# Splitting the last tiles before an output norm, and the start of the next group, into token halves

## The reference

```python
def rms_norm_2(x, gain):
    xf = x.astype(jnp.float32)
    y = xf * lax.rsqrt(jnp.mean(xf * xf, axis=-1, keepdims=True) + RMS_EPS)
    return y.astype(x.dtype) * gain

for l in range(DEPTH):
    h = rms_norm_2(x, g_pre_mix[l])
    m = hybrid_mixer(h, ...)              # ends in  y @ w_out
    x = x + rms_norm_2(m, g_post_mix[l])
    h = rms_norm_2(x, g_pre_ffn[l])
    f = conv_ffn(h, ...)                  # ends in  (gelu(gate) * up) @ w_down
    x = x + rms_norm_2(f, g_post_ffn[l])
```

## Time and profile before

| | |
|---|---|
| median of three runs | 2911.78 us |
| span of the profiled execution | 2910.6 us |
| PE matmuls | 2894.1 us (99%), 14902 |
| PE weight loads | 2395.3 us (82%) |
| DVE | 1819.4 us (63%) |
| ACT | 1275.0 us (44%) |
| POOL | 181.9 us (6%) |
| DMA | 263.90 MB, 27.3% of the engines' time on the weight queue |
| chain that ended last | PE 94%, ACT 2%, DVE 2% |

### The profile page before, as it was taken

How to read it: one execution, slowest core, us unless ns; L and a number is a source line. 1 busy time by engine, 2 the same in 40 slices (tenths; PEclk the granted TensorE clock), 3 DMA queues, 4 the chain that set the end, 5 groups by cost and what they waited for, 6 DMA issues and landing times.

```text
span 2910.6 us, 38306 instructions
## 1 busy us (share of the span) xinstructions
PE 2894.1 (99%) x14902; PEld 2395.3 (82%) x14902; DVE 1819.4 (63%) x3151; ACT 1275.0 (44%) x2352; POOL 181.9 (6%) x124
## 2 busy tenths in 40 slices
PE   9999999999999999999999999999999999999998
PEld 8888888888888888888888788888888888888886
DVE  5766775345555387733657767775365777677743
ACT  4544443333333354432356544543233765444431
POOL 1000000010000000000101301000030022100000
PEclk9999999999999999999999999999999999999999
DMA  4232333322222232232411132333233112323322
GB/s 158 76 102 95 101 96 100 95 87 80 80 85 81 95 101 95 94 101 85 144 60 44 59 102 80 102 99 97 94 106 117 38 52 73 109 76 101 98 94 73
DMA packets 74727, 263.90 MB, mean 91 GB/s; under 512 B 9009, under 2 KB 9009, under 8 KB 74417
## 3 DMA queue, kind: packets, MB, share of 16 engines
q1 hardware_dynamic: 73680, 258.03, 27.3%
q10 hardware_dynamic: 864, 3.41, 0.3%
HBM read 255.64 MB, written 2.10 MB: 89 GB/s over the span
## 4 chain that ended last, share of the span: by engine, by line
PE 94%; ACT 2%; DVE 2%; issue 1%; DMA 0%; POOL 0%; DVEq 0%; SPq 0%
PE bank L551 26%; PE bank L558 26%; PE bank L554 26%; PE bank L760 2%; PE bank L628 2%; PE bank L632 2%; PE bank L629 2%; PE bank L739 2%; PE bank L724 1%; PE bank L930 1%; DVE big L2186 1%; PE bank L715 1%; ACT pp L1157 1%; ACT big L1481 1%; PE bank L983 1%
## 5 line engine op out<-in xcount | busy, mean ns | idle before, releaser
L1502 DVE TENSOR_TENSOR wl<-ring,wh 128x512 fp32r<-128x512 f32 (+1 forms) x928 | 638.6, 694 | 804.8 <-ACT wh L1066 799.5
L551 PE MATMUL bank<-xh,wh 128*128 128x512 f32 x2392 | 943.7, 395 | 0.1
L554 PE MATMUL bank<-xh,wl 128*128 128x512 f32 x2392 | 932.7, 390 | 0.2 <-DVE wl L1502 0.2
L558 PE MATMUL bank<-xl,wh 128*128 128x512 f32 x2392 | 904.5, 390 | 0.0
L1066 ACT ACTIVATE wh<-ring 128x512 fp32r<-128x512 f32 (+1 forms) x928 | 569.1, 622 | 696.6 <-PE bank L558 622.3
L551 PEld LDWEIGHTS bank<-xh,wh 128*128 128x128 f32 x2392 | 449.8, 188 | 102.5 <-issue 10.4
L558 PEld LDWEIGHTS bank<-xl,wh 128*128 128x128 f32 x2392 | 449.3, 188 | 95.0
L554 PEld LDWEIGHTS bank<-xh,wl 128*128 128x128 f32 x2392 | 449.8, 188 | 91.1 <-DVE wl L1502 1.3
L551 PE MATMUL bank<-bigr,wh 128*128 128x512 f32 x1024 | 398.9, 390 | 0.2
L554 PE MATMUL bank<-bigr,wl 128*128 128x512 f32 x1024 | 398.4, 389 | 0.0
L558 PE MATMUL bank<-bigr,wh 128*128 128x512 f32 x1024 | 393.4, 389 | 0.0
(11 more groups left out here) (237 smaller groups left out, 2894.4 us busy)
## 6 DMA issues: line engine op xcount, KB each, us to landing
ring<-in_w_up SPq DMA_DIRECT2D x176, 512.0 KB, 3.5
ring<-in_w_down SPq DMA_DIRECT2D x88, 512.0 KB, 3.5
ring<-in_w_in SPq DMA_DIRECT2D x64, 512.0 KB, 3.6
ring<-in_w_ret SPq DMA_DIRECT2D x32, 512.0 KB, 3.6
ring<-in_w_even SPq DMA_DIRECT2D x19, 512.0 KB, 3.8
ring<-in_w_ret_v SPq DMA_DIRECT2D x16, 512.0 KB, 3.6
ring<-in_w_ret_out SPq DMA_DIRECT2D x16, 512.0 KB, 3.6
ring<-in_w_proj SPq DMA_DIRECT2D x16, 512.0 KB, 3.4
```

Of the source, the lines that this page charges most:

```text
L551: e.matmul(o, K.wh(p, c * 128, 128), oh, start=start, stop=False, skip_group_check=True)
L554: e.matmul(o, K.wl(p, c * 128, 128), oh, start=False, stop=False, skip_group_check=True)
L558: m = e.matmul(o, K.wh(p, c * 128, 128), ol, start=False, stop=stop, skip_group_check=True)
L1502: e.tensor_tensor(K.wl(i, 0, w), K.raw(i), K.wh(i, 0, w).bitcast(F32), ALU.subtract).then_inc(F.lo.tell(("piece", i)), 1)
```

## The change

- `wo` (both layers): tiles 6 and 7 are each computed in two halves of 256 tokens, in the order tile 6 first half, tile 7 first half, tile 6 second half, tile 7 second half, with the same weights twice (`post_out`). The first half's sums and spread stand inside the second halves.
- `down` (both layers): tile 7 is computed in two halves, and its weights come a second time from HBM for the second half (`post_down`).
- ACT's squares, DVE's copies, mean, POOL's root and PE's sums and spread are done for each half.
- The next group does its first three steps (`EARLY`) for the first half of the tokens, then for the second, and the rest as before (`late_group`). The second half's sums stand behind step 0 and its spread behind step 1 of the first half.
- DVE's feed of those three steps goes by halves (`early`), ACT's too.
- The matmuls on constants behind the output norms go, but for the last norm. The far-ahead splitting of pieces goes: `ahead` loses its special case, and `+ 10` becomes `+ 3` with a few pieces put between the halves.
- The last norm, its additions and the output go by halves: sixteen transfers instead of eight. Four small copies of DVE move from before a group to behind it.

The diff, cut to its core:

```diff
     def ahead(self, key):
-        if key[:2] in (("wo", 0), ("wo", 1), ("down", 2)) and key[2] > 5:
-            return self.final[key] + (5 if key[2] == 6 else 8)
         return min([self.final[key] + 3] + ...
...
-        W.stationary(D[f"w_down{f}"], 0, [("down", f, j) for j in range(DT)], FT)
+        W.stationary(D[f"w_down{f}"], 0, [("down", f, j) for j in range(DT + f // 2)], FT)
...
+    def late_group(key, operand, banks, hooks, s):
+        parts = [[take() for _ in banks] for k in range(EARLY)]
...
+        for h in range(2):
+            for k in range(EARLY):
+                oh = operand[0](k, h)[:, side(h)]
+                for m, b in enumerate(banks):
...
+                    high(BK[b][:, side(h)], *parts[k][m], oh, h == 0 and k == 0)
+                ol = operand[1](k, h)[:, side(h)]
+                for m, b in enumerate(banks):
+                    low(BK[b][:, side(h)], *parts[k][m], ol, False, last=h == 1 and parts[k][m][1] == 3)
+                if h == 0 and k == 0:
+                    half_sums(s, 1)
+                if h == 0 and k == 1:
+                    half_spread(s, 1)
+        group(key, DT, operand, banks, hooks, EARLY)
...
+    def post_out(l, operand):
...
+        for i in range(2):
+            half_tile(("wo", l, 6 + i), DT, operand, b[i], 0, [(p, c, False) for p, c in parts[i]])
+        for i, hooks in enumerate(({1: lambda: half_sums(s, 0)}, {0: lambda: half_spread(s, 0)})):
+            half_tile(("wo", l, 6 + i), DT, operand, b[2 + i], 1, [(p, c, c == 3) for p, c in parts[i]], hooks)
...
+    def post_down(l):
+        s, key = ("p", l, "f"), ("down", 2 + l, DT - 1)
+        for h, hooks in enumerate(({}, {1: lambda: half_sums(s, 0), 8: lambda: half_spread(s, 0)})):
...
# ACT, post
-        hi_to(W.final[(*key, DT - 1)] + 10)
+        p = W.final[(*key, DT - both)]
+        hi_to(W.final[(*key, DT - 1)] + 3)
+        if both:
+            half_square(s, key, DT - 2, 0)
+        half_square(s, key, DT - 1, 0)
+        hi_to(p + 4)
+        if both:
+            half_square(s, key, DT - 2, 1)
+        hi_to(p + 6)
+        half_square(s, key, DT - 1, 1)
...
# DVE, post
-        lo_to(W.final[(*key, DT - 1)] + 10)
+        lo_to(W.final[(*key, DT - 1)] + 3)
+        if both:
+            half_copy(s, key, DT - 2, 0, M)
+        half_copy(s, key, DT - 1, 0, M)
+        if not both:
+            lo_to(W.final[(*key, DT)] - 2)
+        half_mean(s, 0)
...
# DVE, post_feed (p: the next group's first piece)
+        def early():
+            if not both:
+                lo_to(p - 2)
+            half_first(0)
+            if both:
+                half_copy(s, key, DT - 2, 1, M)
+            lo_to(p - 1)
+            half_x(0, 0)
+            half_low(0, 0)
+            lo_to(p + 1)
+            half_next(1, 0)
+            lo_to(p + 3)
+            half_mean(s, 1)
+            half_copy(s, key, DT - 1, 1, M)
+            half_low(1, 0)
+            half_next(2, 0)
+            half_low(2, 0)
+            half_first(1)
+            half_x(0, 1)
+            half_low(0, 1)
+            half_next(1, 1)
+            half_next(2, 1)
+            half_low(1, 1)
+            half_low(2, 1)
```

More of the change, by code:

```diff
@@ L513, in sync_program @@
             e.dma_start(K.DIL, K.D["dil"]).then_inc(F.dil.tell("dil", by=16), 16)
[L514 to L521, removed]
+    for h in range(2):
+        for j in range(DT):
+            if j in (1, 3, 5):
+                q.wait_ge(F.pool, ("x", "end", j, h))
+            else:
+                q.wait_ge(F.dve, ("x", "end", j, h))
+            e.dma_start(K.out[:, j * S + 256 * h:j * S + 256 * h + 256], K.x(j)[:, side(h)]).then_inc(
+                F.out.tell(("out", j, h), by=16), 16)
+    q.wait_ge(F.out, ("out", DT - 1, 1))
+    q.wait_ge(F.proj, ("tile", "down", 3, DT - 1, 1))
 def tensor_program(e, q, K):
@@ L653, in sums @@
         vacated[b] = [(F.dve, ("ms", s))]
-        w = 1 if apart is None else 128
         for i in range(NQ):
[L656 to L662, removed]
+            m = e.matmul(BK[b][:, i:i + 1], K.tmp(slot)[:, i * 128:(i + 1) * 128], K.cs("ones", 1), start=i == 0,
+                         stop=i == NQ - 1, skip_group_check=True)
         m.then_inc(F.stat.tell(("sums", s)), 1)
@@ L959, in tensor_program @@
         s = ("n", l)
-        turn[0] = [0, 1, 4, 5, 6, 7]
-        group(("n", l, "g"), DT, xn(s), [next_bank() for _ in range(5)], norm(s, 6, 7) if l else norm(s))
+        if l == 0:
+            turn[0] = [0, 1, 4, 5, 6, 7]
+        banks = [next_bank() for _ in range(5)]
+        if l:
+            late_group(("n", l, "g"), xn(s), banks, norm(s, 6, 7), ("p", 0, "f"))
+        else:
+            group(("n", l, "g"), DT, xn(s), banks, norm(s))
         tile(("n", l, 5), DT, xn(s), F.dve)
@@ L1398, in scalar_program, with half_square @@
     residual(("down", 1), ("n", 0))
+    def half_square(s, key, j, h):
+        q.wait_ge(F.proj, ("tile", *key, j, h))
+        q.wait_ge(F.dve, ("sqa", s, j - 2))
+        e.activation(K.tmp(j % 3)[:, side(h)], K.bank((*key, j, h))[:, side(h)], ACT.Square, bias=0.0, scale=1.0).then_inc(
+            F.act.tell(("sq", s, j, h)), 1)
     def post(s, key, nxt):
-        for j in range(DT):
+        both = key[0] == "wo"
+        for j in range(DT - 1 - both):
             hi_for((*key, j))
@@ L2195, in vector_program, with end_add @@
         post(("p", l, "f"), ("down", 2 + l), XM)
[L2196 to L2206, removed]
+    s, key = ("p", 1, "f"), ("down", 3)
+    def end_add(j, h):
+        q.wait_ge(F.dve, ("m", s, j, h))
+        e.tensor_tensor(K.x(j)[:, side(h)], K.x(j)[:, side(h)], XM[j][:, side(h)], ALU.add).then_inc(
+            F.dve.tell(("x", "end", j, h)), 1)
+    lo_to(W.final["down", 3, DT])
+    for h in range(2):
+        if h:
+            half_mean(s, 1)
+            half_copy(s, key, DT - 1, 1, XM)
+        for j in range(DT):
+            half_m(s, key, j, h, XM, "g_post_ffn_2", 8, XM[j][:, side(h)])
+            if j % 2:
+                end_add(j - 1, h)
+        end_add(DT - 1, h)
 def gpsimd_program(e, q, K):
@@ L2275, in gpsimd_program @@
                 e.tensor_tensor(p, p, K.sp(2 * t + i)[:, 0:width(step)], ALU.subtract).then_inc(F.pool.tell(("p", L, t, i)), 1)
-        root(("p", l, "m"), 64)
+        for h in range(2):
+            half_root(("p", l, "m"), h)
         for j in range(DT):
@@ L2279, in gpsimd_program @@
         root(("f", 2 + l), 224)
[L2280 to L2283, removed]
+        for h in range(2):
+            half_root(("p", l, "f"), h)
+            for j in (1, 3, 5) if l else ():
+                q.wait_ge(F.dve, ("m", ("p", 1, "f"), j, h))
+                e.tensor_tensor(K.x(j)[:, side(h)], K.x(j)[:, side(h)], K.XM[:, j * S + 256 * h:j * S + 256 * h + 256],
+                                ALU.add).then_inc(F.pool.tell(("x", "end", j, h)), 1)
 def constants():
```

201 lines of the change are left out of this document (153 added, 48 removed).

## The result

The changed kernel takes 2920.11 us (median of 6 runs, 2919.05 to 2921.71); the kernel before, in 6 runs beside it, 2911.91. The ratio is 1.0029, with a 95% interval of 1.0018 to 1.0039: slower by 8.2 us. Forecast were 2915 and a range of 2903 to 2921: the result lies inside the range by 0.9 us, and in the slower case, which had a chance of 0.30, not in my own with 0.52.

What follows compares the result with a forecast made beforehand. PE's matmul stream, busy 2894.1 of 2910.6 us, was taken as the bound, with its holes and tail. Three places losing +5.5 and the tail gaining 2.4 made +3.1 on 2911.78: 2914.9 us, range 2903 to 2921.

Steps and rivals of the forecast that it cites:

- the slower case: Whole kernel: the change makes it slower by more than 0.2% (5.8 us); chance 0.30.
- my own: Whole kernel: time stays within 0.2% of before, spanning 2908 to 2917 us, point forecast 2914.9; chance 0.52.
- Halved matmuls: PE in `wo`, `down` and three groups: 363 matmuls become 726 at 0.118 us each, costing 3.3 us in all.
- The hole: PE's 6.01 us wait before a group after `wo` vanishes; PE reaches the group 12.4 us after tile 6 starts.
- Steps 0 to 2: PE at the group's start: the first three steps, done by halves, take 11.9 us instead of 10.4.
- DVE up to m of step 3: DVE early in the group: m of step 3 starts at 22.9 us; PE's first stall is 1 us.
- DVE from there to P+8: DVE inside the group: 13.35 us of work plus 4.25 for five POOL adds at 0.85; split done at 40.5.
- the two rivals on the lock: Inside the group, POOL's adds cost DVE nothing (2902.2 us, chance 0.18) or 1.49 us each (2924.5 us, chance 0.28).
- The dearer rival: Inside the group, DVE waits POOL's whole add, 1.49 us, for each of five: 2924.5 us, chance 0.28.
- The end of the place: Group behind `wo` is over at 47.1 us against 45.3 before, so each such place loses 1.8 us.
- Tail: After the last `down`: final norm and output by halves gain 2.4 us, bounds 1.5 and 3.2.
- Weight loads pace the halves: PE's halved matmuls: 188 ns weight loads set their pace, costing 54 us, giving 2966 us; chance 0.02.

Runs made afterwards that it cites:

- e9_again: The changed kernel itself, run once more with nothing altered: 2922.25 us, ratio 1.0040 to the kernel before.
- e4_halves: The kernel before, with each 512-column matmul of `wo` and the last two `down` stages issued as two of 256 columns: 2930.86 us, ratio 1.0063.
- e3_no_adds: The changed kernel, with POOL's adds of squares inside the groups covering only 2 of 512 columns: 2903.05 us, ratio 0.9970.
- e5_order: The changed kernel, with the split of P+8 (ACT's part likewise) moved ahead of m, x and xl of step 7: 2912.13 us, ratio 1.0002.
- e10_filled: The changed kernel, with six warming matmuls in PE's long wait at step 6 in each of three places: 2918.86 us, ratio 1.0023.

## Why the prediction was off in size and right in mechanism

The mechanism was the one forecast: the hole goes, DVE becomes the bound inside the group, the group ends later than before, and the tail gives part of it back. The result, +8.2, lies beyond the likeliest case's own 2917, in a case that I had only by a dearer lock. That it fell inside the stated range was partly luck: on the chip of e9_again the same kernel's median was 2922.25, outside it. Predicted +3.1; the differences are +4.65 at the places (3.30, 3.55 and 3.30 in place of 5.5 in all) and -0.65 at the tail; the rest, +1.1, I put down to the clock in the first six executions; only the profiled one of them has a trace, with a dip of 3.15.

- *Halved matmuls.* 0.120 in place of 0.118 each (e4_halves): 363 pairs cost 4.8, not 3.3. It is contained in the places and the tail.
- *The hole.* Right. PE reaches the group 12.60 us after the tile's start (12.4 predicted) without a wait.
- *Steps 0 to 2.* 1752.67 to 1765.49, where the stall of 0.78 begins, is 12.82, not 11.9: 0.2 of it from the halves' pitch, 0.3 at the four transposes (0.69 from their start at 1757.20 to the next matmul, which comes when ACT's xh of step 2 is there; predicted 0.4), 0.2 because 1765.49 is the recorded end of a matmul and not the time at which the next could start, the rest in gaps too short for the list of waits. A place without any wait gains 2.05 (e3_no_adds), not 2.9.
- *DVE up to m of step 3.* 23.6 after the tile's start, predicted 22.9: the second mean 0.2 later, 0.3 more of waiting for ACT's xh, 0.2 more work. The stall at step 3 was 0.78 (1 predicted).
- *DVE from there to P+8.* This carries the answer, and it held: 18.2 us against 13.35 + 4.25 = 17.6. Stretched rows against bare ones: +1.05, +1.09, +0.55, +0.56 and +1.07 (the split of P+8 alone takes 1.75) for the five adds that I had counted, 4.32 or 0.86 per add, where I took 0.85. What I had not counted are the second add of the pair before, which still costs the x at 1764.45 0.32, and 0.2 in which DVE waits for ACT's xh of step 7 (the two xl at 1775.76 of e3_no_adds take the same 1.62 as here). Neither of the two rivals on the lock had the price right: not 1.49 per add, and far above 0.25.
- *Why 0.86 and not 1.49.* The dearer rival had the rule right and the price wrong: an operation that meets an add is held to the add's end, but it comes up when part of the add is over (last section).
- *The end of the place.* P+8 at 41.8 instead of 40.5, the spread at 48.6 instead of 47.1. Small misses of one sign (0.7 before m of step 3, 0.6 after it) added up in series, and as the place is the difference of two larger terms (4.3 won at the hole, 7.6 lost in the group; predicted 4.5 and 6.3), they took it from +1.8 to +3.3. The time at which P+8 is split is the term that was mis-sized.
- *The order within the queue.* I took the place of P+8's split as given. e5_order shows that it alone is worth 2.2 us per place. It could be read in the kernel's code: in DVE's `group` the split that PE needs for the third bank of step 6 stands behind the feed of step 7.
- *Tail.* The last add of DVE ends 24.9 us after the tile's start, as predicted (the row at 2916.77: 2917.5 - 2892.63). The output behind it took 2.4 in place of the same 3, 0.6 more gain than the 2.4; that the parts of half the size are the reason is not shown.
- *Doubled weights and moved copies.* Nothing, as forecast: the stages between the places agree within 0.1 us.
- *Clock.* Missed. The prediction had the warming matmuls as mere filling of a hole that goes, and the new stalls as the time they last. The stalls also cost clock: 3.15 us in the profiled execution, and filling the longest stall of each place gave 3.4 of the median on the chip of e10_filled.
- *Weight loads pace the halves.* Out; the pitch is 0.120 against loads of 188 ns.

## What to carry to other kernels

When a change hides a hole on the bound engine, list what the engine that feeds it did inside that hole: here it had split weights ahead, and that work came back in the middle of the next stage, the one with the least room. Then read that engine's queue in order and ask of each item when its reader wants it; moving one split ahead of the last feed gave 2.2 us per place, and moving most of the six into idle time further ahead made the kernel faster than before. A wait on TensorE can cost more than it lasts, so look at the granted clock behind it.

## What the runs showed of the hardware that I had not expected

- *The clock can fall behind short stalls too.* In the 8 us up to 2152.00 PE was busy for 6.28 and idle only in one wait, which lasted 1.92 in all; then it ran at a granted 0.56 for 7.5 us. With the stall filled the 5 us behind it show 1.00. It fell behind `down` in both profiled executions of the changed kernel and in none behind `wo`, with the same stalls; why there is open.
- *POOL's add holds a DVE operation to the add's end.* At all three places, before and after, a 512-column x, xl or split that starts while an add runs ends 0.54 to 0.56 us after the add's recorded end: the split at 1769.08 at 1770.85 (add: 1770.30), the x at 1774.20 at 1775.44 (add: 1774.89). So an add costs what is left of it when the operation comes up, less 0.12 to 0.19: 1.22 left cost the split 1.09, 0.69 left cost the x 0.55. An m, which reads PSUM, kept its 0.73, and while it runs the add goes on. It works the other way too: an add that starts while an x or xl runs ends some 1.15 after it, so that 1.50 or 1.79 is recorded in place of 1.30. The Trainium skill ("SBUF — State Buffer", SBUF: two separate sides) has the shared pair as an exclusive lock in which the other one blocks for the whole instruction. These rows agree.
- *What half width costs on DVE, from start to start.* The prediction compared recorded lengths (0.42 to 0.48 against 0.69 to 0.75). From start to start, in the changed kernel from 1759.71 to 1761.47, a half m, x and xl take 0.51, 0.34 and 0.40, full ones 0.77, 0.61 and 0.67: a halved pair costs 0.25, 0.07 and 0.13 more, on the engine that then decides.
